# A two-block transformer kernel on one core: the keys' stage joined to the third feed-forward layer, compression over 128 rows, gates with weights held, and identity products in eight of TensorE's waits

## The reference

```python
def shared_kv(h, ...):                         # after the feed-forward layer ffn_2
    u = modulate(rms_norm(h, kv_norm_g), shift, scale)
    kv = (u @ w_kv).reshape(b, s, 3, 2, N_KV_HEADS, HEAD_DIM)     # heads 2, width 64
    def compress(t, i):                        # 31 blocks of 32 tokens, stride 16
        blocks = ... + cmp_pos[i]
        flat = blocks...reshape(b, n_c, N_KV_HEADS, 32 * 64)
        return silu(flat @ phi_w1[i]) @ phi_w2[i]                 # hidden 128
    ...
# h = h + 0.5 * gt * swiglu(...)               # then the layer ffn_3
def nsa_mixer(u, k_cmp, v_cmp, k_slc, v_slc, k_win, v_win, w_qg, q_gain, w_o):
    qg = u @ w_qg                              # 1024 columns of queries, 48 of gates
    gates = sigmoid(qg[..., 1024:])
    # three attentions (compressed, selected, window), each weighted by its gate
    o = gb[0] * o_cmp + gb[1] * o_slc + gb[2] * o_win
```

## Time and profile before

| what | value |
|---|---|
| median of 3 runs | 3918.15 us (3917.72 to 3918.2) |
| the profiled execution | 3920.8 us, of it the span 3919.0 us |
| TensorE busy | 3684.9 us, 94% of the span |
| DVE, ACT busy | 1884.6 us (48%), 1390.8 us (35%) |
| mean granted clock of TensorE | 0.956 |
| loads from memory | 357.86 MB, 92 GB/s over the span |

### The profile page before, as it was taken

One profiled execution on the slowest core, in us unless ns is written; L12 is line 12 of the kernel. 1 busy time (PEld: TensorE's weight loads), 2 busy tenths in 40 slices (PEclk: granted clock), 3 DMA queues, 4 the chain that ended last, 5 costly groups with the idle time before them and its releaser, 6 DMA issues.

```text
span 3919.0 us, 49470 instructions
## 1 busy us (share of the span) xinstructions
PE 3684.9 (94%) x19084; PEld 2912.6 (74%) x19084; DVE 1884.6 (48%) x3837; ACT 1390.8 (35%) x2471; POOL 107.3 (3%) x183
## 2 busy tenths in 40 slices
PE   8979999989998999999999989999899998889999
PEld 3458975778887888777777767887788877667887
DVE  4656735566566333555555453334333344764333
ACT  1142212432233222555555543223222232863222
POOL 1100000011111000000000000000000000000000
PEclk9979999989999999999999999999799997999999
DMA  6500015426662222111111112223222221002222
GB/s 251 193 1 1 1 60 193 156 97 220 231 215 104 91 102 84 72 65 49 49 50 65 58 70 86 95 91 105 88 81 95 88 73 44 2 23 86 86 107 76
DMA packets 47299, 362.87 MB, mean 93 GB/s; under 512 B 5232, under 2 KB 5616, under 8 KB 28144
## 3 DMA queue, kind: packets, MB, share of 16 engines
q1 hardware_dynamic: 23616, 272.47, 19.0%
q0 software_dynamic: 23472, 87.50, 6.4%
HBM read 357.86 MB, written 2.10 MB: 92 GB/s over the span
## 4 chain that ended last, share of the span: by engine, by line
PE 84%; DVE 7%; issue 4%; ACT 3%; PEld 1%; DVEq 1%; DMA 0%; PEldq 0%; ACTq 0%; POOL 0%; SPq 0%; POOLq 0%
PE bank L793 20%; PE bank L798 20%; PE bank L799 20%; PE bank L756 5%; PE bank L1591 5%; PE bank L1925 1%; PE bank L1913 1%; PE bank L1942 1%; PE bank L2388 1%; PE bank L774 1%; PE bank L2355 1%; PE bank L1901 1%; PE bank L735 1%; DVE w_lo_sb L1210 1%; PE bank L2377 1%
## 5 line engine op out<-in xcount | busy, mean ns | idle before, releaser
L793 PE MATMUL bank<-x_hi_sb,w_hi_sb 128*128 128x512 f32 x2704 | 1089.7, 403 | 68.1 <-DVE x_lo_sb L1337 20.0
L798 PE MATMUL bank<-x_lo_sb,w_hi_sb 128*128 128x512 f32 x2704 | 1066.4, 394 | 0.0
L799 PE MATMUL bank<-x_hi_sb,w_lo_sb 128*128 128x512 f32 x2704 | 1066.1, 394 | 0.0
L793 PEld LDWEIGHTS bank<-x_hi_sb,w_hi_sb 128*128 128x128 f32 x2704 | 516.0, 191 | 213.3 <-issue 83.9
L1033 ACT ACTIVATE w_hi_sb<-slab_sb 128x1024 fp32r<-128x1024 f32 (+2 forms) x525 | 477.2, 933 | 445.7 <-PE bank L793 258.7
L1210 DVE TENSOR_TENSOR w_lo_sb<-slab_sb,w_hi_sb 128x1024 fp32r<-128x1024 f32 (+2 forms) x525 | 544.6, 1070 | 172.3 <-ACT w_hi_sb L1033 155.2
L799 PEld LDWEIGHTS bank<-x_hi_sb,w_lo_sb 128*128 128x128 f32 x2704 | 515.7, 191 | 111.1
L798 PEld LDWEIGHTS bank<-x_lo_sb,w_hi_sb 128*128 128x128 f32 x2704 | 516.9, 191 | 101.0
L1361 DVE TENSOR_TENSOR hid_sb<-silu_gate_sb,bank 128x512 f32<-128x512 f32 x110 | 75.7, 688 | 625.1 <-PE bank L799 625.1
L793 PE MATMUL bank<-hid_hi_sb,w_hi_sb 128*128 128x512 f32 x880 | 343.3, 390 | 0.0
L799 PE MATMUL bank<-hid_hi_sb,w_lo_sb 128*128 128x512 f32 x880 | 342.9, 390 | 0.0
(11 more groups left out here) (351 smaller groups left out, 3975.3 us busy)
## 6 DMA issues: line engine op xcount, KB each, us to landing
slab_sb<-weights SPq DMA_DIRECT2D x81, 2048.0 KB, 7.7
slab_sb<-weights SPq DMA_DIRECT2D x44, 1536.0 KB, 6.4
keep_sb<-ada POOLq DMA_DIRECT2D x104, 512.0 KB, 4.8
slab_sb<-weights SPq DMA_DIRECT2D x20, 1280.0 KB, 5.9
work_sb<-ada POOLq DMA_DIRECT2D x49, 512.0 KB, 5.5
tables_sb<-ada POOLq DMA_DIRECT2D x7, 512.0 KB, 6.7
h_sb<-x SPq DMA_DIRECT2D x4, 512.0 KB, 7.2
out<-h_sb SPq DMA_DIRECT2D x8, 256.0 KB, 2.0
```

Source lines behind the costliest of these rows:

```text
L793: mm = pe.matmul(e.A.bank[s][:, :], w_hi[p][:, w], hi, start=first, stop=False)
L798: pe.matmul(e.A.bank[s][:, :], w_hi[p][:, w], lo, start=False, stop=False)
L799: return pe.matmul(e.A.bank[s][:, :], w_lo[p][:, w], hi, start=False, stop=last)
```

## The change

Six edits:

1. **Compression over 128 rows.** Pairs of neighbouring positions stand on the two halves of the partitions: ACT writes each tile of `kv_cmp` in four copies (head by odd or even position) in place of one, DVE adds the positions in 8 instructions in place of 4, and one product takes 128 rows and both heads (62 columns): 32 products in place of 128, into one bank. "phi" is one slab in place of two.
2. **The barrier after the keys' stage goes**, and `pe_rms_spread` of ffn_3 moves ahead, to behind the swap of the keys.
3. **Gates with weights held.** The 48 gate columns are the stationary operand and 512 tokens move: 24 products in place of 96, right behind the last query tile. ACT copies the result to SBUF (`gate_rows`), four transposes turn it, ACT copies it again.
4. **Order in "sparse_q".** One settle less; the swap of the first four queries comes after the gates.
5. **Values among the transposes.** In `attend_sparse` the products with the values are cut into shares; the first stands before the wait for the weights, the others between groups of transposes.
6. **Identity products.** `pe_stay_busy(e, n)` issues n fp32 products of the identity with itself into a transposing bank that nobody reads: 20 after the barrier "cross"; 16 after the spread behind "ffn_1"; 4, 5 and 10 (before the last sums, before the spread, after it) behind "dilated_out", "ffn_2", "ffn_3" and "sparse_out"; 20 at the end of "sparse_q"; 16 after "sparse".

```diff
-            pe.matmul(e.A.bank[s][:, :], w_hi[p][:, w], lo, start=False, stop=False)
-            return pe.matmul(e.A.bank[s][:, :], w_lo[p][:, w], hi, start=False, stop=last)
+            pe.matmul(out, w_hi[p][:, w], lo, start=False, stop=False)
+            return pe.matmul(out, w_lo[p][:, w], hi, start=False, stop=last)
...
+        def pe_stay_busy(e, times):
+
+            for _ in range(times):
+                e.eng.matmul(turn_bank[1][:, 0:P], ident, ident, start=True, stop=True)
...
+                        for x in range(total * share // shares, total * (share + 1) // shares):
...
+                    shares = max(groups - 1, 1)
+                    values(0, shares)
                     if 1 <= i <= n:
                         eng.wait_ge(weighed, e.nth(weighed))
                         total = blocks(units[i - 1][1])
                         for at in range(0, total, 4):
+                            if 2 <= at // 4 <= shares:
+                                values(at // 4 - 1, shares)
                             t = e.give(tp, e.tp)
...
             e.stage_end("ffn_2")
+            pe_stay_busy(e, 4)
             pe_sums_close(e)
+            pe_stay_busy(e, 5)
             pe_rms_spread(e)
+            pe_stay_busy(e, 10)
             pe_parts_opening(e, x_hi, x_lo)
...
+            def compress(sl):
+                for i in range(2):
+                    for t in range(16):
+                        mm = pe.matmul(e.S.bank[hidden][:, 64 * i:64 * i + 2 * NCMP],
+                                       sl[:, (16 * i + t) * P:(16 * i + t + 1) * P], kv_blk[:, i, t, :],
+                                       start=t == 0, stop=t == 15)
+                mm.then_inc(e.S.full[hidden], 1)
...
-            pe_slab(e, (), 0, 0, None, more=[compress(0)])
+            pe_slab(e, (), 0, 0, None, more=[compress])
             pe_swap(e, kv_raw, 4)
-            pe_slab(e, (), 0, 0, None, more=[compress(1)])
-            for s in two:
-                pe.drain().then_inc(e.S.full[s], 1)
+            pe_rms_spread(e, False)
...
-            e.stage_end("kv")
-
-            pe_rms_spread(e, False)
             pe_ffn(e)
...
             pe_tile_parts(e)
+            e.slab.next()
+            pe_tile_parts(e, 64, 48)
             pe_settle(e)
             pe_swap(e, q_raw[:, 0:4, :], 4)
-            e.slab.next()
-            pe_token_parts(e, 1, 48, 64, together=True)
-            pe_settle(e)
             pe_head_cols(e, q_sq[:, 4:8, :], 4)
+            pe.wait_ge(copied, e.nth(copied))
+            s = e.give(e.A, e.acc)
+            for b in range(NB):
+                mm = pe.transpose(bank[s][:, b * 48:(b + 1) * 48], gate_rows[0:48, b * P:(b + 1) * P], ident[0:48, 0:48])
...
             pe_swap(e, q_raw[:, 4:8, :], 4)
+            pe_stay_busy(e, 20)
             e.stage_end("sparse_q")
```

More of the change, by code:

```diff
@@ L2312, in go, with end @@
                 self.seat.pos = self.start + self.names.index(name)
+            def end(self):
+                self.seat.pos = self.start + len(self.names)
         def sparse_units():
@@ L2364, in attend_sparse, with values @@
                         scores(i + 1, (1, 2))
-                    if i >= 2:
+                    groups = (blocks(units[i - 1][1]) + 3) // 4 if 1 <= i <= n else 0
+                    def values(share, shares):
+                        if i < 2:
+                            return
                         tile, b = units[i - 2]
-                        kv = tile // 4
-                        if i - 2 in opens:
-                            outs[tile] = e.give(e.A, e.acc)
-                        eng.wait_ge(copied, e.nth(copied))
-                        for x in range(1 + 2 * (b + 1)):
+                        kv, total = tile // 4, 1 + 2 * (b + 1)
+                        if share == 0:
+                            if i - 2 in opens:
+                                outs[tile] = e.give(e.A, e.acc)
+                            eng.wait_ge(copied, e.nth(copied))
+                        mm = None
+                        for x in range(total * share // shares, total * (share + 1) // shares):
                             for hh in heads:
```

107 lines of the change are left out of this document (62 added, 45 removed).

## The result

The changed kernel takes 3897.34 us (median of 5 runs, 3892.99 to 3898.42) against 3917.72 of the kernel before on the same chip (5 runs, 3916.42 to 3918.2): a ratio of 0.9946, 95% interval 0.9935 to 0.9956, some 20 us. The time lies inside the stated range (3866 to 3901) and the direction is right. But 13 us of the forecast gain are missing, and they are missing in one place.

The account below looks back on a forecast made before the run. TensorE's program was taken to bound the kernel, partly below full clock. Savings of 16.0 (keys), 14.3 (gates), 3 (attention's start) and 2.8 (identity products), less 2 (values), made 34.1: 3918.15 to 3884.0 us, range 3866 to 3901.

Parts of the forecast that it names:

- The keys' stage: Compression to first product of ffn_3: 16.0 us saved; 19 with compression and swap at full clock, 9 at half.
- DVE's rotations end just under that cover: Keys' stage: DVE's 7.8 us of key rotations end at 2806.3, just before ACT's finished root at 2807.0.
- no longer ended by a DMA: Keys' stage, sign of being right: ACT's split of ffn_3's slab no longer waits for the slab's load.
- The gates: End of sparse_q: 14.3 us saved, 16.5 if the clock holds, 12 if the swap is at half clock too.
- The start of the attention: First units of attention, 17.0 us at half clock before: 3 us saved, at most 6, at least 0.
- Values among transposes: Attention, 176 of 384 value products moved behind the weights' wait: 2 us lost; bounds 10 saved, 9 lost and more.
- values cost more: Rival, attention: half of the moved 19 us uncovered, 9.5 lost in place of 2; 3892 us, chance 0.12.
- Identity products: Four boundaries 4 us saved, cross 1.2 lost, ffn_1 0.8 lost, sparse 0.8 gained: together 2.8 saved.
- The sign that was named: Four boundaries, sign of being right: PEclk at 1.00 in the first products behind them.
- they do nothing: Rival: identity products hold no clock and cost their own time; 17 us saved in all, 3901 us, chance 0.15.
- the clock then holds nearly everywhere: Rival: compression, swap and spread at full clock, attention 5.5, boundaries 8.7; 49 us saved, 3869 us, chance 0.18.
- The slower rival: Attention loses its clock in the regrouped turns; all 160 us at half clock would give 3964 us, chance 0.02.

Follow-up runs that it names:

- e5: e1 with the barrier after the keys' stage kept and the norm's spread behind it, as before the change: 3878.29 us (one run).
- e1: The changed kernel with all products with the values again before the wait for DVE's weights: 3879.55 us, 0.9907 of before.
- e4: The changed kernel with the values uncut, in one block behind the second group of transposes where the unit has three groups or more: 3902.04 us (one run).
- e3: The changed kernel without any identity product: 3906.48 us, 0.9971 of before.
- e2: The kernel before with only the values cut into shares among the transposes: 3932.81 us, 1.0044 of before.
- e8: e1 with the coming unit's scores against the compressed keys moved between the transposes, in units of three groups or more: 3872.94 us (one run).
- e6: e1 with identity products at three further places: 10 and 24 in the keys' stage, 7 before the second spread of sparse_q: 3872.29 us (one run).
- e7: e1 with fewer identity products behind cross and ffn_1, and other numbers at the four boundaries: 3874.37 us (one run).

## Why the prediction was right, and where it was wrong

**The keys' stage, 16.0 forecast, 18.3 measured: right, by its own steps.** The compression took 7.36 us (8.0 taken), 64 records at 0.115, near the full-height row of 0.124 and not the 0.053 of the half-height form. The load costs by its columns and not by its rows, as the Trainium skill has it (TensorE: Matmul & The Clock Gate, LDWEIGHTS). The trace agrees: at 128 columns a load's record takes 188 ns on average with 64 rows (before) and 192 with 128 (with the change). The 4.5 us that the prediction drew from a quarter of the loads did not come, 7.36 were measured: the old form's records follow each other every 0.053 us at full clock, the new form's every 0.115. The Trainium skill's Part 3 of the same page, by which loads run beside products only in other row groups, agrees with both paces. Swap and spread ran at full clock (3.67 and 1.05; 5.3 and 1.6 taken): most of the 2.3 us by which the term was too small. The slab was off the chain, and what came next was DVE: "DVE's rotations end just under that cover" was off by a little, for they ended last, and the last small products (L2638) waited 2.86 us for the reciprocal behind them. The sign "no longer ended by a DMA" failed by 0.23 us, without a price. Edit 2 is 2.3 of it at the place (e5).

**The gates, 14.3 forecast, 15.2 measured: right step for step.** 24 products took 5.6 us (5.5), the sums 3.63 (3.5), the new wait for the reciprocal 1.95 ("some 2"), the spread 5.02 (6.03, most of what was gained beyond the forecast), and the 20 identity products lay inside the wait: from the last swap's start to the first scores it is 9.09 us with them (3260.76 to 3269.85) and was 9.09 without (3295.84 to 3304.93).

**The start of the attention, 3 forecast, 0.8 measured** (189.03 against e1's 188.2). The gain lies in the first two turns, 19.45 us in place of 20.2. The attention ran at 0.70 in place of 0.50 over its first 17 us, but DVE, busy for 13.93 of them in e1, takes over, as the lower bound of 0 had it.

**Values among transposes, 2 lost forecast, 15.3 to 15.6 measured: the step that failed.** It gave the bounds 10 saved and 9 lost ("and more if nothing fits"), and the truth lies well outside the two figures. Two things were wrong in it. It priced the lost cover by the wait that showed (6.5 us on the row, 9.3 with its twin's), and by a half of the moved 19 us in the rival; but so short a wait behind 50 us of values says that the values already hide most of DVE's time, so that each of them that goes is exposed. e1 and e4 give 19.1 us for 19.4 moved and 28.9 for 27.3. And it had no term for cutting a run in pieces: 0.15 us for each of 42 runs more, some 6 to 7 of the 8.7 us of added busy time. The gain it named, the copies' waits, came whole: 12.4 us. The rival "values cost more" named the mechanism, with 9.5 us.

**Identity products, 2.8 saved forecast, 6.3 in the table** (1.2 of it in the token products), 9 by the medians of e3, in which the attention's clock has a large part. Behind the four boundaries 3.4 against 4; behind "sparse" 2.0 against 0.8, since the half-clock stretch that I had not counted vanished; behind "cross" and "ffn_1" next to nothing, for what the 20 and 16 came late they gained in clock. The sign that was named came: 1.00 in the first products behind all four boundaries. The step is right in kind. That they do nothing is refuted by e3, and that the clock then holds nearly everywhere by the stretches at half clock that are left (the first products behind the keys' stage, the second spread of "sparse_q", the start of the attention).

**The slower rival**, an attention that loses its clock, was given 0.02 with "nothing in the trace points to it". In the changed kernel's trace one turn in the middle lost some clock (0.81), no more, but e3's 211.9 us against e2's 204.35 shows its mechanism at a price of 7.6 us: it was closer than I had it.

The sum: keys +2.3, gates +0.9 and identity products +3.5 beyond the forecast, the attention 15.7 short of it, and the untouched stretches of this pair of traces 2.9 on the other side: 34.1 + 2.3 + 0.9 + 3.5 - 15.7 - 2.9 = 22.2, of 22.4 between the traces.

## What to carry to other kernels

What stands in front of a wait is its cover. Before work is moved behind it, ask how long the wait would be with nothing in front, and take that as the price: a short wait in the profile is a sign of good cover and not of spare time. To fill a gap behind a wait, take work that already stands behind it and that another engine waits for (e8), and keep runs of like products whole. Identity products held the clock where they stood in an empty wait just ahead of large products (e6); of those ahead of a step on the chain, the ones that e7 took away had held nothing.

## What was not expected of the hardware

- **Cutting a run costs TensorE time.** Runs of fp32 products of 64 columns took some 0.15 us beside 0.055 a record, when they alternate with transposes of 128 by 128; 36 runs more added 5.8 us of busy time at full clock (the changed kernel against e1), and none where the runs stayed whole (e4).
- **Behind products of two columns the clock fell, though TensorE was busy.** After 3.63 us of them, and with no wait, the granted clock was 0.50 for 3.4 us (e6). No run takes these products away, so that they are the reason is not shown.
- **The same code gets different clocks.** Behind the same instructions a stretch at half clock was 3.4 us in one trace and 6.8 in another (the changed kernel and the one before, in the token products behind ffn_2), and the same attention was granted 0.94 in e2 and 0.89 in e3. Some of what is gained at one boundary is given back at the next, where such stretches come longer (e7: all of the 1.8 us behind "cross").
